# Layer step on one core: order of loads, copies, squares and state transposes in the program head

## The chip, the cores and the metric

The kernel runs on one core of a Trainium2 chip. The core has five engines that run their own instruction streams and wait for each other on semaphores: PE (TensorE, matrix products and transposes through it), DVE (VectorE), ACT (ScalarE), POOL (GpSimd) and SP (SyncE), which here only issues DMAs. The metric is the device time of one execution in microseconds.

## The reference, cut to what matters

One inference step of a two-layer decoder, for a prompt of 256 tokens and 8 sequences of 8 new tokens (320 columns in all, D_MODEL 1024):

```
for l in range(DEPTH):                                  # 2
    h = rmsnorm(x, norm_mix[l])
    hq, hf, hi, hg, nq, kc, vc, ks, vs, kw, vw, ngate, mgate = split(h @ w_in[l])
    f = lb_l + (1 - lb_l) * sigmoid(hf)                 # forget gates, lb from hg_lower
    a = HGRN2(silu(hq), f, hi, hg)                      # gated linear recurrence, 4 heads of 128
    b = NSA(nq, ...)                                    # attention on compressed, selected, window rows
    x = x + (sigmoid(g_a) * (a W_a) + sigmoid(g_b) * (b W_b)) @ w_out[l]
    h2 = rmsnorm(x, norm_ffn[l])
    x = x + W_down(gelu(causal_conv3(h2 W_gate)) * (h2 W_up))   # state_conv: two old rows per sequence
y = rmsnorm(x, norm_final)
```

The norm is not applied before the input projection: x times the gain is multiplied with the weights, and each result is scaled by rs = 1 / sqrt(mean of squares).

## The kernel before, in words

**Tiles.** xT holds x transposed, as 8 tiles of 128 x 320. Products that need full precision are made of three fast ones: each operand is split into a high part (an ACT copy that rounds) and a low part (a DVE subtraction), and PE sums high x high, high x low and low x high. A unit of weights is 128 x 2048; `split` makes its high part on ACT (work_parts, two buffers in turn) and its low part on DVE (ring_low). `entry_high` and `entry_low` do the same for x times gain, one tile of 8 at a time.

**Weights.** They come through a ring of four slots. SP loads blocks in a fixed order (`BLOCKS`): par, w_hf, w_hq, w_nq, cmp, w_hi, w_kvn, w_kvc and so on; block n + 4 goes into the slot of block n, after a wait that says that block n has been read. SP does this in order, so a load stands behind all loads ahead of it:

```
for n, b in enumerate(BLOCKS):
    ...
        if b == "par":
            sp.wait_ge(cst_ready, L + 1)
        elif b == "cmp":
            sp.wait_ge(rows_ready[L], NSEQ)
        elif b in LAST_USE:
            ...
            sp.wait_ge(*R.filled(LAST_USE[b]))
        ...
        load(BLOCKS[(n + NSLOT) % NBLK], lay + (n + NSLOT) // NBLK)
```

par is the block of small parameters (gains, convolution weights and the old convolution rows, state_conv). The block that follows in its slot, cmp, is 16 pages of the compressed cache, and each page needs its number loaded from SBUF to a register of SP (`page`, `ld`).

**Program head (before layer 0).** PE does six matmuls on zeros, waits for the first constants and for four loads on one semaphore (x of the prompt, x of the samples, hg_lower, norm_final), transposes x tile by tile into the four ax banks of PSUM, then the two small rows ("low") and the parameters ("par"). DVE copies every x tile out. ACT squares each tile (`square_of_x`), splits the first unit of w_hf in between, then makes the high parts of x. POOL adds the eight squares (L2338). DVE subtracts the first unit (`split`, L1729), makes the eight low parts (`entry_low`, L1723), computes the forget bounds lbs from hg_lower, and subtracts the second unit.

**Layer.** PE: the forget tiles hf0 to hf3 (units 0 and 1), with the norm matmul `norm1_sums` in the middle of hf1; the query tiles hq0 to hq3 (units 2 and 3); `nq` tiles with levels 0 to 2 of the recurrence; the transposes of the cached rows (`rows_turned`, 16 for the first four sequences); then hi (block w_hi) between further levels. ACT turns the norm matmul's sums into rs and then loads another activation table for the sigmoids. DVE, in order: bounds, the four transposes of the conv states (L1791; the last one raises cst_ready), clearing of acc (L1931), then per forget tile `forget_in` (L1936, PSUM times rs), after the sigmoid on ACT `forget` (L1940, L1941), with the units 2 and 3 subtracted behind tiles 1 and 3; query tiles; levels. In level 2 it subtracts the first unit of w_hi before it takes the two PSUM banks of that level (`level_take`, L1825, L1830), and these banks are the ones that the third and fourth group of cached rows are transposed into. PSUM banks are given out by `Banks` in the order of a plan; a bank is free when the tile four places earlier has been taken out. Nearly every product has line L713, every PE transpose L716 and every ACT instruction L1364, since helpers issue them.

Of the kernel before, what the change touches and what calls it, by code (L numbers as in the profile page):

```python
# [36 lines left out]
ALU = mybir.AluOpType  # L37
# [36 lines left out]
DMAS.update(par=8, cmp=2 * NSEQ, w_nq=KVH * KD, w_kvc=2, w_cmp=4, kv0=4 * NPAGE + 4, kv1=4 * NPAGE + 4, st0=2, st1=2, br0=3,  # L74
# [93 lines left out]
PRO_PLAN = [(f"x{k}", "V") for k in range(KD)] + [("low", "V")]  # L168
# [66 lines left out]
def hybrid_step(nc, x_prompt, x_sample, cache_cmp, cache_slc, cache_win, state_hgrn, state_conv, page_table, norm_mix,  # L235
# [4 lines left out]
    with ctx:  # L240
# [83 lines left out]
        vX = [part(mixb, at, 512).rearrange("p (u c) -> p u c", u=2) for at in (13568, 11520)]  # L324
        sq = part(mixb, 0, KD * T).rearrange("p (k t) -> p k t", k=KD)
# [96 lines left out]
        landed = [sem(f"ring_landed{s}") for s in range(NSLOT)]  # L422
        pro_full, pro_x, lb_in, lb_exp = sem("pro_full"), sem("pro_x"), sem("lower_in"), sem("lower_exp")
# [26 lines left out]
        exp_ready, scaled, vx_ready = lsem("exp_ready"), lsem("probs_scaled"), lsem("vx_ready")  # L450
        s_ready, sn_ready, sqo_ready = lsem("state_ready"), lsem("new_state"), lsem("o_squares")
        high_rows = lsem("sample_rows_of_high_parts")
        decayed, merged_ready, pre_ready = lsem("state_decayed"), lsem("merged_ready"), lsem("prefix_ready")
        conv_ready, gelu_ready, act_ready = lsem("conv_ready"), lsem("gelu_ready"), lsem("act_ready")
        biased, gated_up, act_hi = lsem("conv_centre"), lsem("act_product"), lsem("act_high")
# [10 lines left out]
        PRO = Banks(PRO_PLAN, axb, pro_full, {"V": pro_x})  # L466
# [11 lines left out]
        def x_tile(l, k):  # L478
            return (x_ready[l - 1], KD + k + 1) if l else (pro_x, k + 1)
# [31 lines left out]
        def _(sp):  # L511
# [12 lines left out]

            def load(b, lay):
                s = slot(b)
                if b == "par":
# [5 lines left out]
                    for y in range(2):  # L533
                        ld(b, s[16 * y:16 * y + 16, 256:256 + DFF // 2], lay1(state_conv, lay)[
                            :, :, :, DFF // 2 * y:DFF // 2 * (y + 1)].rearrange("o b w c -> (o b w) c"))
# [167 lines left out]
        def _(pe):  # L703
# [242 lines left out]
            def state_deltas(h):  # L946

                pe.wait_ge(vx_ready[L], h + 1)
# [159 lines left out]
            def layer(l):  # L1108
# [4 lines left out]
                for h in range(1, HH):  # L1113
                    entry_tile(f"hf{h}", h // 2, h % 2, None, norm1_sums if h == 1 else None)
# [222 lines left out]
            for n in range(6):  # L1337
                mm(mmb[3][:, 0:T], hT[:, 0, 0:P], hT[:, 0, :], True, True)
            pe.wait_ge(first_consts_in, 16)
            pe.wait_ge(xin_in, 64)  # L1340
            for k in range(KD):
                bank = begin(PRO, f"x{k}")
                for i in range(3):
                    last = tr(bank[:, P * i:P * i + TM[i]], xin[0:TM[i], i, P * k:P * k + P])
                last.then_inc(pro_full, 1)
            bank = begin(PRO, "low")
            tr(bank[:, 0:16], attb[0:16, 0:P]).then_inc(pro_full, 1)
            params_turned(0)
# [11 lines left out]
        def _(sc):  # L1360
# [27 lines left out]
            def split(u, l):  # L1388

                if u == 0 or SPLIT[u][0] != SPLIT[u - 1][0]:  # L1390
# [8 lines left out]
            def layer(l):  # L1399
# [36 lines left out]
                def sample_rows_high(out, bank):  # L1436

                    A(out, bank[SMP:P, :], ACT.Copy, scale=rsc[SMP:P, 6:7]).then_inc(*st.up(high_rows[L]))
# [167 lines left out]
                for x, name in enumerate(("op0", "op1", "os0", "os1")):  # L1606
                    bank = take(AXR[L], name)
                    A(oX[x].rearrange("p h v -> p (h v)"), bank[:, :], ACT.Square, scale=HD ** -0.5).then_inc(
                        *st.up(sqo_ready[L]))
# [38 lines left out]
                for j in range(NJ):  # L1648
                    gx, cv = gext[j % 2], cvt[j % 2]
                    sc.wait_ge(*MM[L].emptied_at(f"g{j}"))  # L1650
                    if j >= 2:
# [5 lines left out]
                      **taps).then_inc(*st.up(biased[L]))  # L1657
# [47 lines left out]
        def _(ve):  # L1705
# [29 lines left out]
            V.memset(hT[:, 0, :], 0.0).then_inc(zeros_ready, 1)  # L1735
            V.memset(epsb[:, :], EPS).then_inc(eps_ready, 1)
            for k in range(KD):
# [857 lines left out]
```

## Time and profile before

| | us |
|---|---|
| median of 3 runs | 1139.02 |
| lowest, highest | 1137.69, 1140.99 |
| the profiled execution, its own time | 1140.74 |
| its span | 1139.0 |
| PE busy | 1104.3 |
| DVE, ACT, POOL busy | 727.4, 524.1, 311.1 |

A row of the timeline gives start and duration in microseconds, engine, line, operation, the tile written and those read, how many, and in brackets how long the engine stood before it and what it was released by. A duration of several merged instructions goes from the first one's start to the last one's end. The chain of waits is followed back from the end of the program, each piece with start and duration. DMAs are shown by their issue on SP; the time to landing is asked for apart.

### The profile page before, as it was taken

How to read it: one execution, taken by the hardware profiler on the slowest of the kernel's cores; microseconds unless marked ns; L12 is line 12 of the kernel's file. 1: busy time of each engine (PE TensorE's matmuls, PEld its weight loads, DVE VectorE, ACT ScalarE, POOL GpSimd, SP SyncE). 2: the span in 40 equal slices, each digit the busy share in tenths (PEclk: the TensorE clock that was granted, in tenths of full speed). 3: DMA queues.
4: the chain of work that ended last, by engine and by line, in shares of the span. 5: the costliest groups of instructions: out<-in, count | busy, mean ns of one | idle time of the engine just before them, and what ended most of it. 6: DMA issues, size and time to landing. Idle time of an engine off the chain costs nothing.

```text
span 1139.0 us, 21320 instructions
## 1 busy us (share of the span) xinstructions
PE 1104.3 (97%) x8613; PEld 1031.0 (91%) x8613; DVE 727.4 (64%) x1303; ACT 524.1 (46%) x853; POOL 311.1 (27%) x444
## 2 busy tenths in 40 slices
PE   6999999999999999999999999999999999999997
PEld 5988787889999999999999787777899999999996
DVE  5697175757567777763578844655756677777443
ACT  4543274453355555542444334644434555555232
POOL 3156755323120111100124586432312111110002
PEclk8999999999999999999999999999999999999998
DMA  9565331348644444334455625213784444443321
GB/s 296 139 183 189 119 121 52 112 122 253 210 151 143 153 152 149 117 118 164 148 125 198 197 83 177 75 40 95 224 264 150 144 153 152 154 131 117 130 81 47
DMA packets 151752, 165.94 MB, mean 146 GB/s; under 512 B 31596, under 2 KB 114406, under 8 KB 151398
## 3 DMA queue, kind: packets, MB, share of 16 engines
q1 hardware_dynamic: 151654, 164.58, 46.3%
q8 instruction: 68, 1.11, 0.4%
q14 instruction: 30, 0.25, 0.1%
HBM read 156.16 MB, written 12.46 MB: 148 GB/s over the span
## 4 chain that ended last, share of the span: by engine, by line
PE 87%; DVE 8%; ACT 2%; issue 1%; DMA 1%; SPq 0%; DVEq 0%; ACTq 0%
PE mm L713 62%; PE ax L713 22%; PE ax L716 4%; ACT attb L1364 1%; DVE ring_low L1729 1%; DVE attb L1887 1%; DMA ring<-in_state_conv 1%; DVE sm L1837 0%; DVE attb L2112 0%; DVE h_low L1723 0%; ACT mixb L1364 0%; DVE pcs L2109 0%; ACT work_parts L1364 0%; DVE cstT L1791 0%; DVE mixb L2167 0%
## 5 line engine op out<-in xcount | busy, mean ns | idle before, releaser
L1729 DVE TENSOR_TENSOR ring_low<-ring,work_parts 128x2048 fp32r<-128x2048 f32 (+2 forms) x116 | 257.9, 2225 | 132.3 <-ACT work_parts L1364 131.9
L713 PE MATMUL mm<-h_low,work_parts 128*128 128x320 f32 x1096 | 342.2, 312 | 0.0
L713 PE MATMUL mm<-work_parts 128*128 128x320 f32 (+1 forms) x960 | 304.3, 317 | 8.8 <-DVE h_low L1723 4.5
L1364 ACT ACTIVATE work_parts<-ring 128x2048 fp32r<-128x2048 f32 (+2 forms) x116 | 211.7, 1827 | 153.3 <-PE mm L713 82.8
L713 PE MATMUL mm<-work_parts,ring_low 128*128 128x320 f32 x896 | 276.6, 309 | 0.0
L713 PEld LDWEIGHTS mm<-h_low,work_parts 128*128 128x128 f32 x1096 | 207.3, 189 | 0.3
L713 PEld LDWEIGHTS mm<-work_parts 128*128 128x128 f32 x960 | 181.2, 189 | 12.9 <-issue 5.0
L713 PE MATMUL mm<-act_parts,ring_low 128*128 128x320 f32 x608 | 188.6, 310 | 0.0
L713 PE MATMUL mm<-act_parts,work_parts 128*128 128x320 f32 x680 | 181.0, 312 | 0.0
L713 PEld LDWEIGHTS mm<-work_parts,ring_low 128*128 128x128 f32 x896 | 169.3, 189 | 0.0
L713 PE MATMUL ax<-act_parts,work_parts 128*128 128x320 f32 x544 | 126.3, 310 | 0.6 <-DVE ring L2158 0.6
L713 PEld LDWEIGHTS mm<-act_parts,work_parts 128*128 128x128 f32 x680 | 120.6, 188 | 4.0 <-issue 3.1
L713 PEld LDWEIGHTS mm<-act_parts,ring_low 128*128 128x128 f32 x608 | 115.1, 189 | 0.0
L713 PEld LDWEIGHTS ax<-act_parts,work_parts 128*128 128x128 f32 x544 | 92.1, 188 | 2.5 <-DVE ring_low L1729 2.2
L713 PE MATMUL ax<-act_parts,ring_low 128*128 128x320 f32 x304 | 93.9, 309 | 0.0
L1364 ACT ACTIVATE attb<-attb,prm 128x256 f32<-128x256 f32 x88 | 41.1, 514 | 93.1 <-DVE attb L2253 93.1
L2338 POOL TENSOR_TENSOR mixb<-mixb 128x320 f32<-128x320 f32 x28 | 28.6, 1022 | 131.4 <-ACT mixb L1364 130.7
L1364 ACT ACTIVATE attb<-ax 128x512 f32<-128x512 f32 (+4 forms) x52 | 33.8, 707 | 60.1 <-PE ax L716 54.6
L2492 POOL COPY work<-attb 128x2 f32<-128x2 f32 x44 | 16.4, 372 | 158.6 <-DVE attb L2253 158.6
L713 PEld LDWEIGHTS ax<-act_parts,ring_low 128*128 128x128 f32 x304 | 57.1, 188 | 0.0
L2259 DVE TENSOR_TENSOR attb<-mm,work 128x320 f32<-128x320 f32 x44 | 21.6, 492 | 48.7 <-PE mm L713 48.7
L713 PE MATMUL ax<-mixb 128*64 128x64 f32 (+5 forms) x848 | 47.3, 257 | 0.0
(256 smaller groups left out, 1739.3 us busy)
## 6 DMA issues: line engine op xcount, KB each, us to landing
ring<-in_w_gate_up SPq DMA_DIRECT2D x44, 1024.0 KB, 7.1
ring<-in_w_in SPq DMA_DIRECT2D x10, 2048.0 KB, 9.1
ring<-in_w_in SPq DMA_DIRECT2D x18, 1024.0 KB, 5.5
ring<-in_w_down SPq DMA_DIRECT2D x8, 1536.0 KB, 6.7
ring<-in_w_out SPq DMA_DIRECT2D x4, 2048.0 KB, 12.2
ring<-in_w_down SPq DMA_DIRECT2D x4, 2048.0 KB, 7.9
ring<-in_w_in SPq DMA_DIRECT2D x32, 128.0 KB, 3.7
ring<-in_cache_cmp_kv SPq DMA_DIRECT2D x32, 128.0 KB
```

The source lines that it names most:

```text
L713: return nc.tensor.matmul(out, lhsT, rhs, start=start, stop=stop)
L716: return nc.tensor.transpose(out, in_, ident[0:in_.shape[0], 0:in_.shape[0]])
L1364: return nc.scalar.activation(out, in_, f, **kw)
L1729: V.tensor_tensor(unit_of(u, ring_r), unit_of(u, ring), unit_high(u).bitcast(F32), ALU.subtract).then_inc(*st.up(w_low[l]))
L1887: last = V.tensor_tensor_reduce(prob[:, e, w, 0:nk], bank[:, 256 * w:256 * w + nk], mask, 1.0, -3e38, ALU.add, ALU.max, mx[:, c:c + 1])
L2259: V.tensor_tensor(ut, bank[:, 0:T], rs[:, 0:T], ALU.mult).then_inc(*st.up(mm_dve[L]))
L2338: last = G.tensor_tensor(sq[:, m, :], sq[:, m - 1, :], sq[:, m, :], ALU.add)
L2492: G.tensor_copy(glast_p[:, :, j - 1], gp[:, SEQ:SEQ + 2])
```

## The change

- SP loads, after x, the par block without the conv states, then w_hf in two halves (first 256 columns on a semaphore of their own), then hg_lower and norm_final, then the conv states (semaphore conv_in).
- DVE copies x tiles 0, 2, 4, 6 and ACT 1, 3, 5, 7.
- In layer 0, POOL squares the tiles itself and adds them up as it goes; ACT squares nothing there.
- PE turns the parameters directly after x, does seven more matmuls on zeros, and turns the two small rows last. In layer 0 the norm matmul stands in the middle of hf2.
- DVE subtracts unit 1 before it computes the bounds. In both layers the four transposes of the conv states stand behind the forget gates and the subtraction of unit 3.
- Some semaphores that existed once for each layer exist once.

```diff
+            def load_conv_states(lay):
+                s = slot("par")
+                for y in range(2):
+                    sp.dma_start(s[16 * y:16 * y + 16, 256:256 + DFF // 2], lay1(state_conv, lay)[
+                        ...
+                            "o b w c -> (o b w) c")).then_inc(conv_in, 16)
...
-            sp.dma_start(attb[0:8, 0:P], hg_lower.rearrange("l (h p) -> (l h) p", p=P)).then_inc(xin_in, 16)
-            sp.dma_start(attb[8:16, 0:P], norm_final.rearrange("(k p) -> k p", p=P)).then_inc(xin_in, 16)
+            load("par", 0)
+            first = kt_of("w_hf", KD, 512)
+            for a, s in ((0, first_w_in), (1, landed[BNO["w_hf"] % NSLOT])):
+                sp.dma_start(first[:, :, 256 * a:256 * a + 256], lay1(w_in, 0)[
+                    :, :, C_HF + 256 * a:C_HF + 256 * a + 256].rearrange("o (k p) c -> p (o k) c", p=P)).then_inc(s, 16)
+            sp.dma_start(attb[0:8, 0:P], hg_lower.rearrange("l (h p) -> (l h) p", p=P)).then_inc(low_in, 16)
+            sp.dma_start(attb[8:16, 0:P], norm_final.rearrange("(k p) -> k p", p=P)).then_inc(low_in, 16)
+            load_conv_states(0)
             sp.dma_start(pages[0:1, :], page_table.rearrange("b n -> (b n)").unsqueeze(0)).then_inc(consts_in, 16)
-            load("w_hf", 0)
-            load("par", 0)
             load("w_hq", 0)
...
-                    entry_tile(f"hf{h}", h // 2, h % 2, None, norm1_sums if h == 1 else None)
+                    entry_tile(f"hf{h}", h // 2, h % 2, None, norm1_sums if h == (1 if l else 2) else None)
...
-            pe.wait_ge(xin_in, 64)
+            pe.wait_ge(xin_in, 32)
...
+            params_turned(0)
+            for n in range(7):
+                mm(mmb[3][:, 0:T], zero[:, 0:P], zero, True, True)
             bank = begin(PRO, "low")
+            pe.wait_ge(low_in, 32)
             tr(bank[:, 0:16], attb[0:16, 0:P]).then_inc(pro_full, 1)
-            params_turned(0)
...
-            for k in range(KD):
-                square_of_x(0, k, squares[0])
-                if k == 5:
-                    split(0, 0)
+            for k in range(1, KD, 2):
+                sc.wait_ge(*PRO.filled(f"x{k}"))
+                A(xT[:, k, :], PRO.bank(f"x{k}")[:, 0:T], ACT.Copy).then_inc(pro_x_act, 1)
+            split(0, 0)
...
-            for k in range(KD):
+            for k in range(0, KD, 2):
                 ve.wait_ge(*PRO.filled(f"x{k}"))
                 V.tensor_copy(xT[:, k, :], PRO.bank(f"x{k}")[:, 0:T]).then_inc(pro_x, 1)
+            params_in(0)
+            split(0, 0)
+            ve.wait_ge(pro_x, KD // 2)
+            for k in range(KD):
+                entry_low(0, k)
+            split(1, 0)
             ve.wait_ge(*PRO.filled("low"))
...
-                ve.wait_ge(*landed_at("par", l))
-                if l:
-                    ve.wait_ge(glast_ready, l)
-                for q in range(4):
-                    last = V.transpose(cstT[32 * q:32 * q + 32], quarters(slot("par")[0:32, 256:256 + DFF // 2], q))
-                last.then_inc(cst_ready, 1)
...
                     if h % 2:
                         split(2 + h // 2, l)
+                ve.wait_ge(conv_in, 32 * (l + 1))
+                if l:
+                    ve.wait_ge(glast_ready, l)
+                for q in range(4):
+                    last = V.transpose(cstT[32 * q:32 * q + 32], quarters(slot("par")[0:32, 256:256 + DFF // 2], q))
+                last.then_inc(cst_ready, 1)
...
-                squares_up_to_added(squares[L])
+                if l == 0:
+                    for k in range(KD):
+                        po.wait_ge(*PRO.emptied_at(f"x{k}"))
+                        last = G.tensor_tensor(sq[:, k, :], xT[:, k, :], xT[:, k, :], ALU.mult)
+                        if k:
+                            link(last)
+                            last = G.tensor_tensor(sq[:, k, :], sq[:, k - 1, :], sq[:, k, :], ALU.add)
+                        if k + 1 < KD:
+                            link(last)
+                    last.then_inc(squares_added, 1)
+                else:
+                    squares_up_to_added(squares[L])
```

DVE before, from the last bound of the forget gates (lbl) to the first query tile. The names: cstT the turned conv states, ring_low the low parts of a unit, mixb<-mm a tile taken from PSUM.

```order
L1784 TENSOR_SCALAR lbl<-lbl 128x4
L1791 STREAM_TRANSPOSE cstT<-ring 32x352 x4
L1931 MEMSET mixb 128x768
L1936 TENSOR_TENSOR mixb<-mm,work 128x320 x2
L1940 TENSOR_SCALAR mixb<-mixb,lbl 128x320
L1941 TENSOR_SCALAR mixb<-mixb,lbl 128x320
L1729 TENSOR_TENSOR ring_low<-ring,work_parts 128x8x256
L1936 TENSOR_TENSOR mixb<-mm,work 128x320
L1940 TENSOR_SCALAR mixb<-mixb,lbl 128x320
```

DVE now, from the second of the four forget tiles to the first query tile (L1960).

```order
L1748 TENSOR_TENSOR ring_low<-ring,work_parts 128x8x256
L1950 TENSOR_TENSOR mixb<-mm,work 128x320
L1954 TENSOR_SCALAR mixb<-mixb,lbl 128x320
L1955 TENSOR_SCALAR mixb<-mixb,lbl 128x320
L1950 TENSOR_TENSOR mixb<-mm,work 128x320
L1954 TENSOR_SCALAR mixb<-mixb,lbl 128x320
L1955 TENSOR_SCALAR mixb<-mixb,lbl 128x320
L1748 TENSOR_TENSOR ring_low<-ring,work_parts 128x8x256
L1998 STREAM_TRANSPOSE cstT<-ring 32x352 x4
L1960 TENSOR_TENSOR mixb<-mm,work 128x320
```

The four transposes, and with them cst_ready, have moved past both subtractions of w_hq and all four forget tiles.

POOL before, the first instructions with data and what follows them.

```order
L2338 TENSOR_TENSOR mixb<-mixb 128x320 x7
L2347 MEMSET mixb 128x1280
L2351 COPY row_parts_54<-work_parts 128x6x64
L2351 COPY row_parts_54<-h_low 128x6x64
L2351 COPY row_parts_55<-work_parts 128x2x64
```

POOL now, the same place; rows L2366 are squares, rows L2369 additions, and the pair goes on to the eighth tile.

```order
L2366 TENSOR_TENSOR mixb<-xT 128x320 x2
L2369 TENSOR_TENSOR mixb<-mixb 128x320
L2366 TENSOR_TENSOR mixb<-xT 128x320
L2369 TENSOR_TENSOR mixb<-mixb 128x320
L2366 TENSOR_TENSOR mixb<-xT 128x320
```

Seven instructions have become fifteen.

## Rows read from the trace of the kernel before

**Rows 1.** The page, busy time by engine; PE's waits over the span.

```profile
PE 1104.3 (97%) x8613; PEld 1031.0 (91%) x8613; DVE 727.4 (64%) x1303; ACT 524.1 (46%) x853; POOL 311.1 (27%) x444
...
PE mm L713 <- DVE ring_low L1729: 4.0, 2, 2.2
```

**Rows 2.** Chain of waits, 0 to 60: start, us, what.

```profile
32.35 0.50 DVE mixb L1936
...
36.27 2.30 DVE ring_low L1729
...
38.62 3.79 PE mm L713 x24
```

**Rows 3.** Timeline, PE: x transposes, first product of hf0, norm matmul.

```profile
8.17 4.62 PE L716 MATMUL ax<-consts,mixb 128*128 128x128 f32 x24 [1.04 <-DMA attb<-in_norm_final]
...
20.34 0.61 PE L713 MATMUL mm<-work_parts 128*128 128x320 f32 x1 [4.45 <-DVE h_low L1723]
...
26.96 0.70 PE L713 MATMUL ax<-mixb,consts 128*128 128x320 f32 x2
```

**Rows 4.** Timeline, DVE, 0 to 75.

```profile
16.44 2.69 DVE L1729 TENSOR_TENSOR ring_low<-ring,work_parts 128x2048 fp32r<-128x2048 f32 x1
19.05 4.38 DVE L1723 SCALAR_TENSOR_TENSOR h_low<-xT,prm,work_parts 128x320 fp32r<-128x320 f32 x8
...
29.21 2.18 DVE L1791 STREAM_TRANSPOSE cstT<-ring 32x352 f32<-32x352 f32 x4
...
42.72 2.29 DVE L1729 TENSOR_TENSOR ring_low<-ring,work_parts 128x2048 fp32r<-128x2048 f32 x1 [2.06 <-ACT work_parts L1364]
...
72.77 0.73 DVE L1825 COPY_PREDICATED mixb<-consts,ax 128x512 f32<-128x512 int32 x1
```

**Rows 5.** Timeline, ACT: first weight split, table load before the sigmoids.

```profile
13.70 1.91 ACT L1364 ACTIVATE work_parts<-ring 128x2048 fp32r<-128x2048 f32 x1 [1.03 <-DMA ring<-in_w_in]
...
28.75 1.28 ACT L1364 ACT_TABLE_LOAD   x1
```

**Rows 6.** Timeline, POOL: the first two additions of squares, and the last.

```profile
10.46 1.80 POOL L2338 TENSOR_TENSOR mixb<-mixb 128x320 f32<-128x320 f32 x2 [10.01 <-ACT mixb L1364]
...
17.05 2.79 POOL L2338 TENSOR_TENSOR mixb<-mixb 128x320 f32<-128x320 f32 x1
```

**Rows 7.** Timeline, layer 1's entry: DVE and POOL at the same time.

```profile
570.23 0.77 DVE L1723 SCALAR_TENSOR_TENSOR h_low<-xT,prm,work_parts 128x320 fp32r<-128x320 f32 x1
...
571.32 0.54 DVE L1723 SCALAR_TENSOR_TENSOR h_low<-xT,prm,work_parts 128x320 fp32r<-128x320 f32 x1
...
571.41 1.20 POOL L2338 TENSOR_TENSOR mixb<-mixb 128x320 f32<-128x320 f32 x1 [0.76 <-ACT mixb L1364]
```

**Rows 8.** Timeline, SP, both layers; issue to landing of the DMA at 51.92.

```profile
32.48 19.40 SPq L515 DMA_DIRECT2D ring<-in_cache_cmp_kv  x16
51.92 20.41 SPq L515 DMA_DIRECT2D ring<-in_w_in  x4
...
583.12 19.46 SPq L515 DMA_DIRECT2D ring<-in_cache_cmp_kv  x16
...
DMA to landing us min/median/max: 8.0/8.0/8.0
```

**Rows 9.** Chain of waits: cached rows and w_hi's tile, layers 0 and 1.

```profile
72.85 1.90 PE ax L716 x16
74.75 7.42 PE mm L713 x32
...
626.17 7.42 PE mm L713 x32
```

**Rows 10.** Layer 1: transposes on DVE, hq0 in the chain, granted clock after it.

```profile
579.11 2.18 DVE L1791 STREAM_TRANSPOSE cstT<-ring 32x352 f32<-32x352 f32 x4
...
588.51 5.33 PE mm L713 x24
...
589.80:593.20 3.40, 3.40 (x15) 3.40 (x14) 1.35 (x4) 2.63 (x3) 0.00 (x0) 0.50 0.33 96
```

More of the change, by code:

```diff
@@ L167 @@
 MM_PLAN, AX_PLAN = mm_plan(), ax_plan()
-PRO_PLAN = [(f"x{k}", "V") for k in range(KD)] + [("low", "V")]
+PRO_PLAN = [(f"x{k}", "VA"[k % 2]) for k in range(KD)] + [("low", "V")]
 END_AX_PLAN = [("sums", "A"), ("y4", "A"), ("y5", "V")]
@@ L324, in hybrid_step @@
         vX = [part(mixb, at, 512).rearrange("p (u c) -> p u c", u=2) for at in (13568, 11520)]
+        zero = part(work, 0, T)
         sq = part(mixb, 0, KD * T).rearrange("p (k t) -> p k t", k=KD)
@@ L422, in hybrid_step @@
         landed = [sem(f"ring_landed{s}") for s in range(NSLOT)]
+        first_w_in, pro_x_act = sem("first_weights_in"), sem("pro_x_by_act")
+        low_in, conv_in = sem("low_in"), sem("conv_states_in")
         pro_full, pro_x, lb_in, lb_exp = sem("pro_full"), sem("pro_x"), sem("lower_in"), sem("lower_exp")
@@ L478, in x_tile @@
         def x_tile(l, k):
-            return (x_ready[l - 1], KD + k + 1) if l else (pro_x, k + 1)
+            return (x_ready[l - 1], KD + k + 1) if l else PRO.emptied_at(f"x{k}")
         down_units = [u for u, (b, _, _) in enumerate(SPLIT) if b[:2] == "dn"]
@@ L532, in load @@
                     ld(b, s[0:32, P:2 * P], lay1(cmp_pe, lay).rearrange("o v (j a) d -> (o v j) (a d)", a=2))
-                    for y in range(2):
-                        ld(b, s[16 * y:16 * y + 16, 256:256 + DFF // 2], lay1(state_conv, lay)[
-                            :, :, :, DFF // 2 * y:DFF // 2 * (y + 1)].rearrange("o b w c -> (o b w) c"))
+                    if not isinstance(lay, int) or lay:
+                        load_conv_states(lay)
                 elif b == "cmp":
@@ L946, in state_deltas @@
             def state_deltas(h):
-                pe.wait_ge(vx_ready[L], h + 1)
+                pe.wait_ge(vx_ready, HH * L + h + 1)
                 for y in range(2):
@@ L1345, in _ @@
                 last.then_inc(pro_full, 1)
+            params_turned(0)
+            for n in range(7):
+                mm(mmb[3][:, 0:T], zero[:, 0:P], zero, True, True)
             bank = begin(PRO, "low")
+            pe.wait_ge(low_in, 32)
             tr(bank[:, 0:16], attb[0:16, 0:P]).then_inc(pro_full, 1)
-            params_turned(0)
             for l in range(DEPTH):
@@ L1388, in split @@
             def split(u, l):
-                if u == 0 or SPLIT[u][0] != SPLIT[u - 1][0]:
+                if u == 0 and l == 0:
+                    sc.wait_ge(first_w_in, 16)
+                    sc.sem_inc(spare, 1)
+                elif u <= 1 and l == 0 or u == 0 or SPLIT[u][0] != SPLIT[u - 1][0]:
                     sc.wait_ge(*landed_at(SPLIT[u][0], l))
@@ L1436, in sample_rows_high @@
                 def sample_rows_high(out, bank):
-                    A(out, bank[SMP:P, :], ACT.Copy, scale=rsc[SMP:P, 6:7]).then_inc(*st.up(high_rows[L]))
+                    A(out, bank[SMP:P, :], ACT.Copy, scale=rsc[SMP:P, 6:7]).then_inc(*st.up(high_rows))
                 def cached_rows(tiles):
@@ L1733, in final_gain @@
                 V.tensor_scalar(hT[:, k, :], xT[:, k, :], pro[:, 8 + k:9 + k], None, ALU.mult).then_inc(end_h, 1)
-            V.memset(hT[:, 0, :], 0.0).then_inc(zeros_ready, 1)
+            V.memset(zero, 0.0).then_inc(zeros_ready, 1)
             V.memset(epsb[:, :], EPS).then_inc(eps_ready, 1)
-            for k in range(KD):
+            for k in range(0, KD, 2):
                 ve.wait_ge(*PRO.filled(f"x{k}"))
                 V.tensor_copy(xT[:, k, :], PRO.bank(f"x{k}")[:, 0:T]).then_inc(pro_x, 1)
+            params_in(0)
[4 more added lines that the diff above has]
+            split(1, 0)
             ve.wait_ge(*PRO.filled("low"))
             V.tensor_copy(pro[:, :], PRO.bank("low")[:, 0:16]).then_inc(pro_x, 1)
-            params_in(0)
-            split(0, 0)
-            ve.wait_ge(pro_x, KD + 1)
-            for k in range(KD):
-                entry_low(0, k)
+            ve.wait_ge(pro_x, KD // 2 + 1)
             def link(ins):
@@ L1767, in _ @@
             link(V.tensor_tensor(lbs[:, 36:40], lbs[:, 28:32], lbs[:, 12:16], ALU.subtract))
-            split(1, 0)
             def layer(l):
```

26 lines of the change are left out of this document (13 added, 13 removed).

## The prediction

> **What bounds the kernel now.** I read the page's first part, then PE's waits: PE is busy for 97% of the span, and the stretches in which it stands are few [rows 1]. So only what lengthens or shortens such a stretch counts. The change edits the head of layer 0 and, through the state transposes, both layers. The chain of waits says what ends last there. PE has done the four forget tiles and stands 2.15 us until the third low part of the weights (DVE at 36.27) is written; from 38.62, the first query tile hq0, it runs on without a gap [rows 2]. Call x the start of hq0. DVE is what is late before x, and the reader should see in [rows 4] why: the first subtraction waits for the turned parameters until 16.44, eight low parts of h follow, a second subtraction, and four transposes of the conv states (2.18 us) directly ahead of the forget gates. PE's norm matmul (26.96, [rows 3]) is not late: rs is there before 28.75, where ACT loads its sigmoid table [rows 5], while DVE first takes a forget tile at 32.35 [rows 2].
>
> **Head: what comes earlier.** The x transposes start at 8.17, 1.04 us after the warm-up matmuls, on two small loads that no longer count [rows 3]. With those gone they start between 7.13 and 8.17; no row has the landing of x alone; I take 7.5, since the small loads were queued directly behind x. They last 4.6 us at PE's pace (8 tiles in 4.62), so copying them by two engines gains nothing. The last x copy on ACT (0.5 us, as DVE's) ends at 12.7. The first weight half, 1 MB with only x and 0.1 MB ahead of it, should have landed by about 11 to 12 (before: 2 MB by 13.70, [rows 5]). ACT then splits 12.7 to 14.6 (1.91), DVE subtracts from about 14.6 instead of 16.44. The parameters are off the path: loaded ahead of the weights, turned at 12.1, copied by 13.
>
> **Head: what GpSimd's squares cost.** Before, 7 adds; now 8 squares and 7 adds on GpSimd, all linked. One takes 0.86 us and 0.94 start to start: 15 x 0.94 = 14.1, from 8.7 (x0 copied) to 22.8, if nothing disturbs. But the add at 17.05 took 2.79 us: it stood until DVE's subtraction (to 19.13) was done, and that subtraction had taken 2.69 instead of 2.29 since it began during an add [rows 4, 6]. In layer 1 the two kinds alternate: h_low at 570.23 takes 0.77, the next one at 571.32 takes 0.54 and makes the add at 571.41 take 1.20 [rows 7]. So they exclude each other. From these rows an add holds DVE for 0.67 (17.05 add: free again at 18.98, h_low's 1.144 us from 19.05 begin in earnest at 19.65), an h_low holds GpSimd for 0.42. With the add always pending, a pair takes 1.09 us, where h_low alone had 0.46 from start to start (4.38 for 8 less one long first). At 14.6 GpSimd has begun 7 ops; 8 are left, one per DVE op: the subtraction 15.1 to 17.3, then h_low k begins at 17.9 + 1.09k, the last at 25.5. That is the price: 8 x (1.09 - 0.46) = 5.0 us on DVE. It cannot be below zero, as GpSimd gives DVE no work away (the squares came from ACT, which was not late).
>
> PE follows DVE: hf0 ends 26.6, hf1 3.5 later at 30.1, and the norm matmul, moved from the middle of hf1 to the middle of hf2, runs at 32.0 (squares ready at 25.7, no wait). rs is ready 1.8 later at 33.8 (before 26.96 to 28.75, [rows 3, 5]). DVE meanwhile subtracts (26.0 to 28.2), does the bounds (2.0), and has no transposes: free at 31.8, so rs binds and the 2.2 us taken away in layer 0 gain nothing. Now ACT's table load (1.28, [rows 5]) stands between rs and the first sigmoid; it was hidden. From the first sigmoid to x it takes what it took before: it began half a us after the forget tile of 32.35, so 32.88 to 38.62, 5.7 [rows 2]. x = 33.8 + 1.3 + 5.7 = 40.8 against 38.62: **+2.1**. Bounds: with no exclusion rs would be at 29.1 and x at 36.2 (-2.4); with PE at its lower clock in hf1 or a full extra wait, +4.
>
> Here the Trainium skill, "SBUF — State Buffer", section "SBUF: two separate sides", says the pair shared by DVE and GpSimd is an exclusive lock for the whole instruction, and that a DVE op with two SBUF inputs is held by a GpSimd op that reads SBUF. The rows agree that they exclude, but give 0.67 and 0.42 held of 0.86 and 0.54. By whole instructions a pair would take 1.40 and the head would end 2.5 us later than I sum.
>
> **The transposes and SP's queue.** They also release the slot of the parameter block. SP waits for that (cst_ready), then issues 16 page loads in 19.4 us (32.48 to 51.92, each with a register load), and only then the loads of w_hi and w_kvn, which stand behind them in SP's order [rows 8]. Now the transposes come after the third and fourth subtraction: 42.72 + 2.29 + 2.18 is x + 8.5 instead of 31.4. Then: first page load x + 9.6 (1.1 later, as before), w_hi issued x + 29.1, landed x + 37.1 (8.0, [rows 8]), ACT's split x + 39.0, DVE's subtraction x + 41.3. PE takes up w_hi (tile hi0) at 74.75, which is x + 36.1 [rows 9]. There is more: DVE, in order, holds behind that subtraction the taking of the two banks of level 2 (72.77, [rows 4]; 0.41 + 0.73 + 0.42 after the subtraction), which the third and fourth group of cache-row transposes on PE (the 16 at 72.85) need empty. So hi0 starts at x + 43.3: PE stands **7.2** in layer 0. The page block itself lands at x + 31 and its rows are made before PE needs them, so w_hi is what binds. The transposes now hold DVE 2.2 us in front of the query tiles; what that costs PE is inside the 7.2, since hi0 waits for SP's chain either way.
>
> Layer 1 has the same order. There the chain of waits runs through the transposes (579.11, 2.18 us), and nothing else holds the forget gates: with them and the short gap behind them gone DVE is 2.4 earlier, and PE's wait of 1.9 before hq0 at 588.51 (the 4.0 of [rows 1] less 2.15) goes [rows 10]. But hi0 is then bound at 588.5 - 2.4 + 43.3 = 629.4 against 626.17 [rows 9]: **+3.2**, that gain included.
>
> **Clock.** After PE stood 1.9 us before 588.51, its clock was granted at half (1.2 GHz) for the 3.4 us from 589.8 (PEclk 0.50), and the 24 matmuls took 5.33 instead of 3.79 [rows 2, 10]; before hf0 it stood longer (4.45 at 20.34, [rows 3]), and there too it began at the lower level. Both new waits are longer (5 to 7 us). I add 1.5 for each, **+3.0**; bounds 0 and 2 x 2. The seven new dummy matmuls only keep PE busy until 16.3, ahead of a paced hf0, and cost nothing: PE waits for DVE there. The semaphores that become one for both layers add no instruction on a path: 0.
>
> **Sum.** 2.1 + 7.2 + 3.2 + 3.0 = 15.5 us. The profiled execution took 1140.7 (span 1139.0), 0.15% over the median 1139.0; against the median that gives 1154.5.
>
> **Rivals.**
> 1. *Head good, queue late.* GpSimd finds room between DVE's ops and x comes at 36.2 to 38.6. For: the first two adds ran in 1.80 beside DVE's copies from PSUM, undisturbed [rows 6]. Against: [rows 6, 7]. 1139.0 - 2.4 to 0 + 7.2 + 3.2 + 3.0 = 1150 to 1152.
> 2. *Everything worse.* Exclusion by whole instructions, or hf1 at the lower clock: +2.5 to +4 more, 1157 to 1159.
> 3. *Faster.* The transposes leave both layers' path and the late loads vanish in slack. Place: w_hi's low part at PE. Price: head -2.4, layer 1 -1.9 and the half clock -1.5 saved: 1133.2. It decides at cst_ready: up to x + 1.3 the queue is in time, the program has x + 8.5. SP would have to issue 16 page loads in 12 us instead of 19.4; both layers' rows speak against it.
> 4. *No difference.* As 3, but with GpSimd's exclusion in the head: +2.1 - 3.4, 1137.7. The same against it. The rival that the change doesn't do what it says falls here: the program's order shows the moves.
>
> **How the numbers follow.** Forecast 1154.5: 0.62. Rival 1: 0.16. Rival 2: 0.09. Rival 3: 0.08. Rival 4: 0.05. 0.3% (3.4 us) is what a measurement of this kernel tells from no change. Faster by more 0.08, within 0.05, slower 0.87. The range goes from 1146.5 (rival 1 without the clock's price) to 1159.5 (rival 2); what is left out is rivals 3 and 4 and a little of the tails.
>
> **What would show it.** h_low on DVE at 1.1 us spacing beside GpSimd ops, last one near 25.5; norm matmul near 32; x near 40.8; no ACT idle between rs and the sigmoids but the table load. SP's page loads starting near 50 and, in layer 1, near 596; ACT waiting for the page block and then for w_hi; PE standing about 7 and 5 us, with DVE's subtraction or its bank copies as releaser, ahead of hi0; half clock behind each. It is wrong if the page loads issue faster than 1.2 us each, if w_hi lands in under 8 us behind them, or if ACT's and DVE's part of w_hi isn't what PE waits for.

## The result, and the profile after

| | before | after |
|---|---|---|
| median of 4 runs | 1138.36 | 1161.47 |
| lowest, highest | 1137.39, 1140.99 | 1160.21, 1163.97 |
| profiled execution, its own time | 1140.74 | 1160.21 |
| its span | 1139.0 | 1158.4 |

The kernel before has one execution more here than in the section ahead. The ratio is 1.0189, with a 95% interval of 1.0174 to 1.0205: the change costs 23 us where 15.5 were forecast, and the time is 2 us above the range. PE's busy time has grown too, although 14 instructions more are no reason for 10 us:

```profile
PE 1114.5 (96%) x8627; PEld 1037.6 (90%) x8627; DVE 724.9 (63%) x1299; ACT 522.0 (45%) x849; POOL 316.1 (27%) x452
```

PE's waits over the span (us in total, times, longest), to be read against [rows 1]. The first line did not stand there before: two waits for the bank taken in level 2 (L1839, L1825 before), one in each layer.

```profile
PE ax L729 <- DVE mixb L1839: 14.2, 2, 7.4
...
PE mm L726 <- DVE h_low L1742: 3.3, 8, 1.2
PE mm L726 <- DVE ring_low L1748: 2.8, 1, 2.8
```

SP's timeline, answering [rows 8]. The page loads start at 49.52 and 608.91, and take as long as before; the first load after them is w_hi.

```profile
49.52 19.41 SPq L518 DMA_DIRECT2D ring<-in_cache_cmp_kv  x16
68.97 9.89 SPq L518 DMA_DIRECT2D ring<-in_w_in  x4
...
608.91 19.61 SPq L518 DMA_DIRECT2D ring<-in_cache_cmp_kv  x16
```

ACT's timeline in layer 0 (in brackets the idle time before, and its releaser): the page block at 71.17, then w_hi at 77.25, each waited for.

```profile
71.17 4.29 ACT L1380 ACTIVATE mixb<-ring 128x512 f32<-128x512 f32 x8 [11.81 <-DMA ring<-in_cache_cmp_kv]
77.25 1.91 ACT L1380 ACTIVATE work_parts<-ring 128x2048 fp32r<-128x2048 f32 x1 [1.80 <-DMA ring<-in_w_in]
```

DVE's timeline: the eight low parts of h (4.38 in [rows 4]), the transposes (29.21 there), w_hi's subtraction and the bank behind it in layer 0, and the subtraction in layer 1.

```profile
17.17 8.09 DVE L1742 SCALAR_TENSOR_TENSOR h_low<-xT,prm,work_parts 128x320 fp32r<-128x320 f32 x8
...
46.27 2.17 DVE L1998 STREAM_TRANSPOSE cstT<-ring 32x352 f32<-32x352 f32 x4
...
79.20 3.17 DVE L1748 TENSOR_TENSOR ring_low<-ring,work_parts 128x2048 fp32r<-128x2048 f32 x1 [6.20 <-ACT work_parts L1380]
...
82.70 0.70 DVE L1839 COPY_PREDICATED mixb<-consts,ax 128x512 f32<-128x512 int32 x1
...
638.80 2.29 DVE L1748 TENSOR_TENSOR ring_low<-ring,work_parts 128x2048 fp32r<-128x2048 f32 x1 [7.47 <-ACT work_parts L1380]
```

PE's timeline at hq0, and the chain of waits, head and hi0 (start, us, what). In [rows 9] the 16 transposes took 1.90 and hi0 7.42; here 8 of them take 1.97 and hi0 8.45.

```profile
39.96 0.63 PE L726 MATMUL mm<-work_parts 128*128 128x320 f32 x1 [2.83 <-DVE ring_low L1748]
...
31.31 0.55 PE ax L726 x2
...
32.93 1.28 ACT L1380
...
37.62 2.29 DVE ring_low L1748
...
83.46 1.97 PE ax L729 x8
85.43 8.45 PE mm L726 x32
```

The reason, in windows (stretch, its length, busy time and instructions of PE, PEld, DVE, ACT, POOL, then PEclk): four stretches at 1.2 GHz that the trace of before doesn't have. Before has two of its own: 16.3 to 23.1 in the head, where DVE is what is late, and the one from 589.8 [rows 10]. A further one, at 760.4 in before and 800.9 in after, costs both the same.

```profile
39.80:43.20 3.40, 3.24 (x12) 3.24 (x13) 2.21 (x7) 2.64 (x5) 0.00 (x0) 0.50 0.00 0
80.70:87.60 6.90, 4.14 (x14) 3.67 (x15) 5.34 (x6) 3.29 (x4) 0.00 (x0) 0.51 1.21 297
135.30:138.80 3.50, 3.50 (x26) 3.17 (x28) 0.26 (x1) 1.23 (x2) 3.25 (x10) 0.51 0.02 5
637.10:647.30 10.20, 5.12 (x16) 4.41 (x17) 6.14 (x7) 7.21 (x6) 1.25 (x1) 0.50 1.16 324
```

**Where the time goes.** I laid the same matmuls of both traces side by side and read off by how much each starts later. Layer 0: hq0 +1.3 (38.62, now 39.96); +1.6 in the half clock behind it; +6.8, the wait; +2.0 half clock on the transposes and hi0 (1.0 each, chain above); +1.5 in the stretch from 135.3. Layer 1: -3.6 (1.9 of waiting before hq0 and 1.7 of half clock behind it, [rows 10], are gone); +7.4, the wait; +2.4 half clock behind it. Sum 19.4, the difference of the spans. The medians lie 23.1 apart: the profiled execution of before stood 2.4 above its median, that of after 1.3 below. The granted clock explains such differences in part: another execution of after had a mean of 0.977 and a span of 1162.2, the profiled one 0.983 and 1158.4, but the two others had 0.983 as well and spans of 1159.5 and 1159.9.

### The profile page after: what moved, and what is told of

It is laid out like the page before. It is cut to its first block, busy times and chain, and to the rows that moved or that the text cites. A ratio compares the mean times of both kernels' runs of the same rounds, so it can differ in the third digit from the quotient of the medians.

```text
span 1158.4 us, 21351 instructions
## 1 busy us (share of the span) xinstructions
PE 1114.5 (96%) x8627; PEld 1037.6 (90%) x8627; DVE 724.9 (63%) x1299; ACT 522.0 (45%) x849; POOL 316.1 (27%) x452
## 4 chain that ended last, share of the span: by engine, by line
PE 78%; DVE 10%; issue 4%; ACT 4%; SPq 1%; POOL 1%; DMA 1%; DVEq 0%; ACTq 0%; POOLq 0%
PE mm L726 54%; PE ax L726 20%; PE ax L729 4%; DVE ring_low L1748 2%; ACT work_parts L1380 1%; ACT attb L1380 1%; DVE attb L1901 1%; SPq L518 1%; POOL mixb L2394 1%; DMA ring<-in_w_in 1%; DVE h_low L1742 1%; SPq L522 1%; ACT mixb L1380 1%; DMA mixb<-in_x_sample 1%; POOL mixb L2409 0%
## 5 line engine op out<-in xcount | busy, mean ns | idle before, releaser
L1380 ACT ACTIVATE attb<-ax 128x512 f32<-128x512 f32 (+4 forms) x52 | 33.8, 697 | 48.4 <-PE ax L729 42.9
L2358 POOL TENSOR_TENSOR mixb<-mixb 128x320 f32<-128x320 f32 x21 | 20.7, 985 | 119.9 <-ACT mixb L1380 119.6
L2394 POOL TENSOR_TENSOR mixb<-mixb 128x1024 f32<-128x1024 f32 (+1 forms) x10 | 33.3, 3326 | 59.1 <-PE ax L726 58.7
```

The lines of the kernel that those rows point to most:

```text
L1380: return nc.scalar.activation(out, in_, f, **kw)
L2358: last = G.tensor_tensor(sq[:, m, :], sq[:, m - 1, :], sq[:, m, :], ALU.add)
L2394: G.tensor_tensor(kL[:, :, 0:ts], kH[:, :, 0:ts], rH[:, :, 0:ts], ALU.mult).then_inc(*st.up(kl_ready[L]))
```

## The experiments

Each time stands with the ratio to the kernel before in the same runs (1139.68, 1139.45 and 1139.36 us in the three sets) and its interval. Theory Q is the prediction's: the late transposes hold SP's queue, and w_hi in it.

### Transposes early again

```diff
...
+                for q in range(4):
+                    last = V.transpose(cstT[32 * q:32 * q + 32], quarters(slot("par")[0:32, 256:256 + DFF // 2], q))
+                last.then_inc(cst_ready, 1)
                 link(V.memset(acc[:, :, :, :], 0.0))
...
                     if h % 2:
                         split(2 + h // 2, l)
...
-                for q in range(4):
-                    last = V.transpose(cstT[32 * q:32 * q + 32], quarters(slot("par")[0:32, 256:256 + DFF // 2], q))
-                last.then_inc(cst_ready, 1)
```

> The changed kernel with one part undone: in both layers the four transposes of the conv states stand again ahead of the forget gates (before the clearing of acc). Theory Q (the late transposes hold SP's 16 page loads and with them w_hi): the waits of 6.8 us (layer 0) and 7.4 us (layer 1) ahead of hi0 go, with the half clock behind each (2.0, 1.5 and 2.4 us); the short gap before layer 1's hq0 comes back (3.7 with its clock). What stays is the head's +1.3 and the half clock behind it (1.8): 1138.4 + 1.3 to 3.1 = 1139.7 to 1141.5 us. DVE was idle 1.87 us where the transposes now stand, so layer 0's hq0 starts at 39.9 to 40.3 as in the changed kernel. Rival H (the head with GpSimd's squares carries a good part of the loss): the time stays above 1148. Page loads on SP start near 33.5 instead of 49.5.

Measured: 1142.83, ratio 1.0025 (1.0014 to 1.0037). Of the 1.89% lost, 0.25% stays; rival H falls. The time is 1.3 us above the top of what was expected. SP's timeline:

```profile
33.53 19.54 SPq L518 DMA_DIRECT2D ring<-in_cache_cmp_kv  x16
```

hq0 was expected at 39.9 to 40.3 and started at 41.65. The profiled execution, at 1145.84, was among the slowest of twelve. DVE isn't the reason for the late start; it still stood for rs after the transposes. PE ran hf0 and hf1 at half clock (window below), so the norm matmul came at 33.00 instead of 31.31, and rs with it.

```profile
22.20:29.10 6.90, 6.84 (x23) 6.07 (x24) 6.42 (x13) 0.21 (x1) 2.58 (x3) 0.51 1.29 226
```

### Transposes late in the kernel before

```diff
...
-                for q in range(4):
-                    last = V.transpose(cstT[32 * q:32 * q + 32], quarters(slot("par")[0:32, 256:256 + DFF // 2], q))
-                last.then_inc(cst_ready, 1)
                 link(V.memset(acc[:, :, :, :], 0.0))
...
+                for q in range(4):
+                    last = V.transpose(cstT[32 * q:32 * q + 32], quarters(slot("par")[0:32, 256:256 + DFF // 2], q))
+                last.then_inc(cst_ready, 1)
                 for h in range(HH):
                     query_in(h)
```

> The kernel before with one part done alone: in both layers the four transposes of the conv states stand behind the forget gates and the fourth subtraction. Theory Q: by the prediction's working with x = 38.6 - up to 1 us (in layer 0 DVE is 2.2 us earlier in the forget gates, but the third low part waits for ACT): page loads from x + 9.6, w_hi's low part on PE 6.8 us late in layer 0 and 7.4 in layer 1, half clock behind both; 1138.4 + 19.4 - 1.3 - 1.8 = 1154.7, range 1150 to 1157. Rival H: under 1148. Rival M (the two parts need each other, DVE free of transposes brings x forward by 2 us and with it the whole queue): 1148 to 1151.

Measured: 1156.53, ratio 1.0153 (1.0133 to 1.0172). This one part makes four fifths of the loss. PE's waits show it, and nothing of the new head is in this kernel:

```profile
PE ax L716 <- DVE mixb L1819: 15.2, 2, 7.7
```

PE no longer stands ahead of hq0, which starts at 36.7, 1.9 earlier than before (the third low part was ready at 36.1); hi0 is late all the same. So the part does what it is for, and SP's queue takes it back. And against this kernel the new head makes hq0 3.3 us later, not 1.3: after loses 0.36% more.

### Squares on ACT, transposes late and early

```diff
                 A(xT[:, k, :], PRO.bank(f"x{k}")[:, 0:T], ACT.Copy).then_inc(pro_x_act, 1)
-            split(0, 0)
+                square_of_x(0, k - 1, squares[0])
+                if k == KD - 1:
+                    split(0, 0)
+                square_of_x(0, k, squares[0])
...
-                        last = G.tensor_tensor(sq[:, k, :], xT[:, k, :], xT[:, k, :], ALU.mult)
...
+                squares_up_to_added(squares[L])
```

> The changed kernel with the squares of layer 0 back on ACT (ACT still copies x tiles 1, 3, 5, 7; POOL only adds): ACT's first weight split comes at about 14 instead of 12.94, but DVE's h_low are spaced 0.46 us instead of 1.0 for most of the eight. Exclusion theory (E): the last h_low ends at 22 to 23 instead of 25.3, layer 0's hq0 at 37 to 38 instead of 39.9, and everything behind it moves with it, the waits ahead of hi0 stay: 1161.5 - 2 to - 3 = 1158.5 to 1159.5. Rival (the spacing comes from ACT's high parts or PE, not from GpSimd): hq0 stays at 39.9 or comes later by the 1 us that ACT loses, 1161.5 to 1162.5.

> The changed kernel with both parts undone (transposes ahead of the forget gates, squares on ACT). Theories Q and E together: the two losses add up, so 1161.5 - (gain of turn_early) - (gain of act_squares) = 1137.5 to 1139.5; layer 0's hq0 at 37 to 39 (DVE has the 2.2 us of transposes back where it no longer waits for rs). What is left against the kernel before is the order of the head's loads and the norm matmul in hf2: -1 to +1.5 us. Rival: with the transposes early the head no longer matters, both_undone equals turn_early within 1 us.

Measured: 1157.70, ratio 1.0152 (1.0134 to 1.0170), and with the transposes early as well 1141.90, 1.0013 (0.9999 to 1.0027). DVE's low parts and, from the chain of waits, PE's products up to the norm matmul, of the first:

```profile
18.07 4.38 DVE L1745 SCALAR_TENSOR_TENSOR h_low<-xT,prm,work_parts 128x320 fp32r<-128x320 f32 x8
...
19.36 10.59 PE mm L726 x60
```

4.38 against 8.09: GpSimd's squares cost DVE 3.7 us there. They start 0.9 later, as ACT has more to do, and end 2.8 earlier. Only 1.4 of that reach the norm matmul (29.95 against 31.31) and hq0 (38.6): from its first product at 19.36 PE runs on without a gap and is itself what is late, with the half clock from 19.6 to 23.1. The waits ahead of hi0 stay at 14.2. With the transposes early the gain is within the measurement's error (1.0025 to 1.0013). This missed the 1137.5 to 1139.5 that were expected: if the two gains added up, the ratio would be 0.9988, and it is 1.0013. The rival, that the time equals turn_early's within 1 us, is what came out; why the gain of the squares all but goes there is open.

### Transposes in the middle

```diff
                     if h % 2:
                         split(2 + h // 2, l)
+                    if h == 1:
...
+                        for q in range(4):
+                            last = V.transpose(cstT[32 * q:32 * q + 32], quarters(slot("par")[0:32, 256:256 + DFF // 2], q))
+                        last.then_inc(cst_ready, 1)
```

> The changed kernel with the four transposes between the second and the third forget tile, right behind the subtraction of unit 2 (both layers). This tests the prediction's due time: cst_ready may come up to x + 1.3 (x is the start of hq0), and here it comes at x + 2.2, so SP's chain is 0.9 to 1.5 us late in layer 0 and not 6.8. Theory Q: page loads on SP from about 43.2, w_hi issued near 62.7 and landed near 70.8, PE standing 0.5 to 1.5 us ahead of hi0 in each layer, layer 1's hq0 without a gap: 1161.5 - 2 x 6 for the waits - 2 to 4 for the clock = 1145 to 1148. Rival (a fixed cost of having the transposes anywhere behind the first forget tile): within 3 us of the changed kernel.

Measured: 1142.50, ratio 1.0023 (1.0010 to 1.0035), better than the 1145 to 1148 that the prediction's rule gave. SP's timeline and PE's waits:

```profile
43.68 19.41 SPq L518 DMA_DIRECT2D ring<-in_cache_cmp_kv  x16
...
PE ax L729 <- DVE mixb L1839: 0.3, 1, 0.3
```

Here cst_ready came at x + 2.0 (42.6; x is 40.56), 5.8 us earlier than after, and the two waits, 14.2 in sum, shrank to 0.3. So the due time is a limit up to which lateness costs nothing, and the x + 1.3 of the prediction was about 1 us too strict: PE itself came later to hi0, having run at half clock behind hq0.

### w_hi ahead of the page loads

```diff
-                for n, b in enumerate(BLOCKS):
+                for n in (1, 0, *range(2, NBLK)):
+                    b = BLOCKS[n]
...
+                split(HIU, l)
                 sc.wait_ge(*landed_at("cmp", l))
...
-                split(HIU, l)
```

> The changed kernel, transposes late as they are, but SP takes its first two steps of a layer in the other order: w_hi is loaded as soon as the forget tiles have been read, and only then SP waits for cst_ready and issues the 16 page loads; ACT splits w_hi's first unit ahead of the page block's copies. Theory Q says that nothing but w_hi's place behind the page loads costs the time: w_hi issued near 40, landed by 50 to 60, the page rows ready from 71.7 on, which is ahead of PE (75 to 76.6), so both waits ahead of hi0 shrink from 6.8 and 7.4 to under 1 us, and their half clock goes; layer 1's hq0 keeps its gain of 3.7: 1161.5 - 14.2 - 4 to 6 = 1141 to 1144, at or below the kernel with the transposes early. Rival P (the page block itself is as late as w_hi): the waits stay over 4 us, 1153 to 1158.

Measured: 1139.33, ratio 0.9995 (0.9985 to 1.0005), below the 1141 to 1144 expected, with all else as in after, the late transposes too. SP and ACT:

```profile
38.23 0.37 SPq L518 DMA_DIRECT2D ring<-in_w_in  x1
50.47 19.77 SPq L518 DMA_DIRECT2D ring<-in_cache_cmp_kv  x16
...
66.45 1.92 ACT L1381 ACTIVATE work_parts<-ring 128x2048 fp32r<-128x2048 f32 x1 [5.98 <-PE mm L727]
72.42 4.29 ACT L1381 ACTIVATE mixb<-ring 128x512 f32<-128x512 f32 x8 [4.06 <-DMA ring<-in_cache_cmp_kv]
```

The page block is as late as in after and nobody waits: both 7 us waits are gone from PE's list. That is the cause, isolated: not that the transposes are late, but that w_hi stands behind what they release. The edit on SP and the one on ACT were not run apart.

### Matmuls that fill the wait

```diff
                 for q in range(4):
+                    if q == 2:
+                        fill = begin(MM[L], "hi0")
+                        for n in range(40):
+                            mm(fill[:, 0:T], h_high[:, 0, 0:P], h_high[:, 0, :], True, True)
                     rows_turned(q)
```

> The changed kernel with 40 matmuls more (128x320, same operands, result overwritten) on PE in each layer where it stands ahead of the last 8 cached-row transposes: 40 x 0.148 = 5.9 us at the full clock, so the waits of 6.8 and 7.4 us are filled and nothing is delayed. Theory C (the half clock behind a wait comes from PE standing): hi0 starts at the same time as in the changed kernel but at 2.4 GHz: -2.0 us in layer 0, -2.4 in layer 1, perhaps -1.5 for the dip at 135.3: 1161.5 - 4.4 to 5.9 = 1155.6 to 1157.1. Rival (the lower clock has nothing to do with the wait, it comes at some place anyway): 1161.5 within 1 us, with dips elsewhere.

Measured: 1158.40, ratio 1.0154 (1.0139 to 1.0170): 0.35%, about 4 us, less than after (3.1 by the medians), by 80 matmuls more. Expected were 4.4 to 5.9. Chain and windows:

```profile
79.52 5.86 PE mm L726 x40
85.37 0.87 PE ax L729 x8
86.25 7.42 PE mm L726 x32
...
76.00:100.00 24.00, 24.00 (x196) 21.10 (x195) 14.34 (x12) 11.21 (x10) 11.08 (x7) 1.00 0.73 211
635.00:660.00 25.00, 22.95 (x152) 19.63 (x150) 15.57 (x14) 10.93 (x9) 8.47 (x7) 1.00 0.65 183
```

The bank comes no earlier (84.7 against 83.4), and the fill ends 0.6 behind it, but transposes and hi0 take 0.87 and 7.42 instead of 1.97 and 8.45. In layer 1 PE still stood for 2.0 us behind the fill, and no half clock followed. So the half clock behind the two long waits came from PE standing there, and it is some 4 of the 23 us. The stretch from 135.3 is missing in this kernel too, so a part of the gain may be its.

### Head or queue: five more

before_hi_first is the kernel before with the two edits shown above, transposes ahead of the query tiles and w_hi first. norm_in_hf1 is w_hi_first with this line changed, and act_sq_hi_first has the squares on ACT as well:

```diff
-                    entry_tile(f"hf{h}", h // 2, h % 2, None, norm1_sums if h == (1 if l else 2) else None)
+                    entry_tile(f"hf{h}", h // 2, h % 2, None, norm1_sums if h == 1 else None)
```

best_acc_later is act_sq_hi_first with the first edit below; best_no_fill has the second one too:

```diff
-                link(V.memset(acc[:, :, :, :], 0.0))
...
                         forget(h - 1)
+                    if h == 1:
+                        link(V.memset(acc[:, :, :, :], 0.0))
```

```diff
-            for n in range(7):
-                mm(mmb[3][:, 0:T], zero[:, 0:P], zero, True, True)
```

> The kernel before with its own head, the transposes behind the forget gates in both layers, and w_hi ahead of the page loads on SP and on ACT. This separates what the late transposes are worth once the queue is out of the way from what the new head is worth. Theory Q: layer 0's hq0 about 2 us earlier (36.6 in the run with the late transposes alone), layer 1's gap and half clock gone (3.7), no waits ahead of hi0: 1139.4 - 3 to - 5.5 = 1134 to 1136.5. Rival N (the gain of act_sq_hi_first comes from the new head, halves and two copying engines): 1138 to 1140.

> The run w_hi_first (GpSimd squares, transposes late) with one edit more: the norm matmul of layer 0 back in the middle of hf1. The prediction says that its move to hf2 makes rs late (33.8) and exposes ACT's table load. If so: rs near 30 instead of 33.4, and hq0 then bound by DVE (bounds end at 30.2, clearing of acc to 31.1, first forget tile there): hq0 at 38 to 38.5 instead of 40, 1139.3 - 1.5 to - 2 = 1137.3 to 1137.8; with a half clock behind hq0 gone perhaps 1 more. Rival (the forget tiles are late for another reason, DVE's work): no change, 1139.3 within 0.7.

> The changed kernel with three edits: squares of layer 0 on ACT, norm matmul of layer 0 back in the middle of hf1, and w_hi ahead of the page loads on SP and on ACT as in the run w_hi_first; the transposes stay late. If the causes found are the whole story this keeps what is good of the change (no transposes ahead of the forget gates: 3.7 us in layer 1) and drops what costs: layer 0's hq0 at 35 to 36.5 against 38.62 before, no waits ahead of hi0: 1138.4 - 2 to - 3 in the head - 2 to - 3.7 in layer 1 = 1131.7 to 1134.4. Rival (a new bound behind, as the level chain on DVE and POOL in layer 1): 1136 to 1140.

> act_sq_hi_first with one edit: DVE clears acc (0.70 us and 0.23 of waiting) between the second forget tile and the subtraction of unit 2, where it stood idle for 1.79 us, and not ahead of the first forget tile, where it held the forget gates. Theory D (DVE's work between h_low and the first forget tile sets hq0 there): hq0 0.9 us earlier, the wait of 0.8 us ahead of it gone: 1134.6 - 0.8 = 1133.8. Rival: no difference.

> best_acc_later without the seven matmuls on zeros that the change adds in the program head. The prediction took them as worth nothing, as PE waits for DVE there: same as best_acc_later within 0.7 us. Rival C (they hold up the clock for hf0): 1 to 2 us slower than best_acc_later, hf0 at the lower level for longer.

| kernel | us | ratio | interval | hq0 at |
|---|---|---|---|---|
| before_hi_first | 1136.03 | 0.9966 | 0.9954 to 0.9978 | 38.2 |
| norm_in_hf1 | 1137.25 | 0.9978 | 0.9966 to 0.9989 | 39.3 |
| act_sq_hi_first | 1134.62 | 0.9955 | 0.9943 to 0.9968 | 36.1 |
| best_acc_later | 1134.73 | 0.9955 | 0.9942 to 0.9969 | 36.8 |
| best_no_fill | 1135.57 | 0.9967 | 0.9955 to 0.9979 | 36.4 |

With the queue out of the way the late transposes are a gain of 0.34% in the old head (before_hi_first); w_hi first with the transposes early was not run, but in before PE had no wait ahead of hi0 that it could take away. The new head on top, as the change has it, loses 0.29% (w_hi_first, 0.9995). The norm matmul's place makes 0.17% of that, with intervals that just overlap: with it in hf1 the wait of 2.8 before hq0 is 0.3 in PE's waits of norm_in_hf1:

```profile
PE mm L727 <- DVE ring_low L1749: 0.3, 1, 0.3
```

GpSimd's squares cost another 0.23% (0.9978 to 0.9955), again with intervals that just overlap. What remains of the new head (halves, two copying engines, order of the small loads) may give 0.1% back (0.9966 to 0.9955), which is within the error. Clearing acc elsewhere brought nothing: hf0 and hf1 were at half clock in its profile and rs came at 29.3, so there was no idle head for it to win. The seven matmuls on zeros are open: 0.12% apart, with intervals that overlap. act_sq_hi_first is faster than both kernels: 0.45% under before, 2.3% under after. It was expected a little faster still (1131.7 to 1134.4), as was best_acc_later (1133.8), and norm_in_hf1's hq0 at 38 to 38.5, not 39.3.

## Why the prediction was right, and why it fell short

The sum's four terms, measured in the spans:

| term | said | measured |
|---|---|---|
| head, hq0 | +2.1 | +1.3 |
| queue, layer 0 | +7.2 | +6.8 |
| layer 1, up to hi0 | +3.2 | +3.8 (-3.6, +7.4) |
| clock | +3.0 | +7.5 (1.6, 2.0, 1.5, 2.4) |

**SP's queue: right, step by step.** Transposes end at x + 8.5 (48.44; x = 39.96), page loads at x + 9.6, w_hi issued at x + 29.0, ACT done with it at x + 39.2 (x + 39.0 said), bank free at x + 43.4 (x + 43.3 said; its own terms, x + 41.3 and 0.41 + 0.73 + 0.42, give x + 42.9). Two things were missed that both make hi0 later: DVE's subtraction took 3.17, not 2.3, as a GpSimd operation of 1.54 us had begun at 78.68, and hi0 doesn't start when the bank comes free, since eight transposes on PE come first (0.87 at the full clock). The wait is 6.8 and not longer because PE came to it 1.6 late, by the half clock behind hq0; that 7.2 came so near is in part luck. In layer 1 PE stood 7.4 where about 5 were foretold: the half clock behind hq0, 1.7, went with the wait before it, so PE was there earlier.

**Head: direction right, but made of two larger parts.** Foretold was x = 40.8, measured 39.96. The x transposes started at 7.94, not 7.5; the last low part ended at 25.3, the norm matmul stood at 31.3 (32.0 said), the table load was exposed as said. The parts: the old head without transposes gives hq0 at 36.7, so taking them away is worth 1.9 there, and the new head costs 3.3. The +1.3 is also a favourable case: the four other kernels with this head and GpSimd's squares (turn_mid, w_hi_first, clock_fill, turn_early) had hq0 at 40.6, 41.0, 41.5 and 41.7, each with a stretch of half clock in the head that after's profiled execution lacks. "The 2.2 us taken away gain nothing" holds for the new head alone, in which DVE waits for rs.

**The exclusion.** The price on DVE was 3.7 us (8.09 against 4.38) where the sum had 5.0: a pair took 1.00 and not 1.09 us, and the subtraction ahead of the low parts hardly paid (2.37 us). The Trainium skill, "SBUF — State Buffer", section "SBUF: two separate sides", has the lock for the whole instruction. A pair would then be 0.54 and 0.72 to 0.86, that is 1.26 to 1.40. The trace doesn't agree for these short operations: the reported durations overlap by some 0.3 to 0.4 us a pair. For the long one it nearly does: a subtraction begun at 79.20 that stood until GpSimd was done at 80.22, and then took its 2.29, would end at 82.51, and it ended at 82.37.

**Clock: the term that failed.** It was +3.0, 1.5 for each new wait, from one row of 3.4 us at half clock behind a wait of 1.9 [rows 10]; measured were 7.5. Behind the two longer waits the stretches are 6.9 and 10.2 us long and cost 4.4. The other 3.1 stand at places where the prediction put nothing: hq0, whose wait went from 2.2 to 2.8, has a stretch too, though it had none before [rows 2], and one more came at 135.3. That the cause is PE standing is shown for the two long ones by the run that fills them. The stretch behind hq0 goes with its wait: all seven profiled kernels that stood 2.8 us before layer 0's hq0 have it, and none of the seven others. The one at 135.3 is not shown to come from the change. In the spans the clock is the whole miss of 3.9: the other three terms were 12.5 and measured 11.9. The rest of the miss is the step from profile to median: the sum was made against the profiled execution of before, 1140.7, and the two profiled executions lie 19.5 apart, the medians 23.1. What makes up these 3.6 us stays open, since one execution of each kernel is profiled. Two places could: the head's stretch of half clock that after's profiled execution lacks, and the 1.7 behind layer 1's hq0 in before's, which turn_early lacks behind the same wait (last section).

**Rivals.** 3 and 4 fell by SP's rows: the page loads take 19.1 us or more in every kernel. w_hi_first takes away what they hang on, and its time is that of the kernel before within the error, rival 4's outcome. 1 is out by hq0 at 39.96. 2 came nearest in time, but its reasons aren't in this trace: pairs of 1.00 us, and hf1 at the full clock. Its second one did come in turn_early, with hf0 and hf1 at half clock and hq0 at 41.65.

## What to carry to other kernels

A step that releases a buffer has a due time: count from its semaphore through everything that the queue behind it must issue, to the engine that needs the last of it. Move such a step only together with the queue's order; here two lines of order on SP and one on ACT turned a loss of 1.9% into none. And price a wait of the bounding engine at more than its length: 14.2 us of standing here cost some 4 us more at the lower clock. Waits of under 3 us did so too, but not each time, so take the price from several traces and not from one row.

## What was not expected of the hardware

The same wait can be followed by half clock in one kernel and not in another. PE stood 1.89 us before layer 1's hq0 in before, both_undone and turn_early; in the first two 3.4 us at PEclk 0.50 and 0.51 followed, in turn_early none. Its timeline and window:

```profile
596.50 0.42 PE L726 MATMUL mm<-work_parts 128*128 128x320 f32 x1 [1.89 <-DVE ring_low L1748]
...
597.80:601.20 3.40, 3.40 (x29) 3.37 (x28) 1.35 (x4) 2.64 (x3) 0.00 (x0) 1.00 0.32 102
```

A wait of 0.28 us for the same ACT instruction was followed by half clock in after (from 135.3, PEclk 0.51 above), turn_early and both_undone, and by none in before, turn_mid, w_hi_first and act_sq_hi_first. PE's timeline and the window of before:

```profile
123.59 0.63 PE L716 MATMUL ax<-consts,mixb 128*128 128x128 f32 x4 [0.28 <-ACT mixb L1364]
...
122.00:125.50 3.50, 3.22 (x35) 2.55 (x36) 0.49 (x1) 2.50 (x5) 3.25 (x7) 1.00 0.02 5
```

And in the head of every profiled kernel but after a stretch of 3.4 to 17 us at half clock fell somewhere between 10 and 29 us, at different places. A stretch of 3.4 us is worth 1.5 to 1.7, more than several of the edits tested. What decides whether a short wait is followed by one stays open. GpSimd's square of a tile, with one tile read twice, took 0.72 us undisturbed, its addition of two tiles 0.86; beside DVE's low parts 0.85 and 1.00:

```profile
18.98 0.85 POOL L2366 TENSOR_TENSOR mixb<-xT 128x320 f32<-128x320 f32 x1
19.91 1.00 POOL L2369 TENSOR_TENSOR mixb<-mixb 128x320 f32<-128x320 f32 x1
```
